# Side work queued by products, and three of four sums of weight quarters made by adding transfers, in a three-layer fp32 block kernel

## The reference

```python
h = rms_norm(x, pre_norm[layer])
c_b, c_c, c_x, c_z, r_q, r_k, r_v, r_z = split(h @ w_in[layer])      # 8 x 1024 columns
y_conv = c_b * causal_depthwise_conv(c_c * c_x, conv_w[layer]) * silu(c_z)
q, k = apply_rotary(r_q), apply_rotary(r_k)                          # 8 heads of 128
ret = retention_chunkwise(q, k, r_v, log_gamma)                      # chunks of 128 tokens
y_ret = ret * rsqrt(mean(ret * ret) + eps) * silu(r_z)
x = x + rms_norm(concat(y_conv, y_ret) @ w_out[layer], post_norm[layer])
```

## Time and profile before

| | us |
|---|---|
| median of 3 runs | 1948.93 |
| lowest, highest | 1947.12, 1953.82 |
| profiled execution, its own time | 1956.33 |
| its span | 1954.2 |

### The profile page before, as it was taken

How to read it: one execution, slowest core, us unless ns; L and a number is a source line. 1 busy time by engine, 2 the same in 40 slices (tenths; PEclk the granted TensorE clock), 3 DMA queues, 4 the chain that set the end, 5 groups by cost and what they waited for, 6 DMA issues and landing times.

```text
span 1954.2 us, 32772 instructions
## 1 busy us (share of the span) xinstructions
PE 1861.4 (95%) x13846; PEld 1760.0 (90%) x13846; DVE 1385.4 (71%) x2461; ACT 903.4 (46%) x1731; POOL 1.2 (0%) x9
## 2 busy tenths in 40 slices
PE   8999999999999999998999999998998898989898
PEld 7999999777999989996889999997898898989887
DVE  5888896577666744666787878876378868786854
ACT  5223333677544422434355555555356455545442
POOL 0000000000000000000000000000000000000000
PEclk9999999999999999999999999998999899999999
DMA  5222222110222232322222222222222222222231
GB/s 183 87 87 87 87 88 86 44 44 22 87 93 87 71 121 90 100 70 83 74 74 78 87 87 87 87 87 87 87 87 66 65 87 80 94 66 87 87 117 67
DMA packets 151856, 163.91 MB, mean 84 GB/s; under 512 B 3494, under 2 KB 148191, under 8 KB 151710
## 3 DMA queue, kind: packets, MB, share of 16 engines
q1 hardware_dynamic: 151694, 161.82, 25.8%
q10 hardware_dynamic: 16, 0.00, 0.0%
HBM read 159.71 MB, written 2.10 MB: 83 GB/s over the span
## 4 chain that ended last, share of the span: by engine, by line
PE 77%; DVE 15%; ACT 5%; issue 2%; DMA 0%; DVEq 0%; SPq 0%; ACTq 0%
PE ps L195 63%; PE ps L199 12%; DVE wlo L210 4%; PE ps L204 2%; ACT ones_d L207 2%; ACT whi L207 1%; DVE raw L210 1%; DVE pa L210 1%; DVE xa L218 1%; DVE sz L218 1%; DVE xa L210 1%; DVE na L210 1%; DVE na L218 1%; DVE rcol L218 1%; DVE s1t L210 1%
## 5 line engine op out<-in xcount | busy, mean ns | idle before, releaser
L210 DVE TENSOR_TENSOR wlo<-raw,whi 128x1024 fp32r<-128x1024 f32 (+1 forms) x352 | 417.1, 1192 | 335.8 <-ACT whi L207 334.8
L207 ACT ACTIVATE whi<-raw 128x1024 fp32r<-128x1024 f32 (+1 forms) x352 | 359.7, 1032 | 227.8 <-PE ps L195 205.4
L195 PE MATMUL ps<-nhi,whi 128*128 128x256 f32 (+3 forms) x1824 | 401.0, 288 | 11.1 <-DVE wlo L210 7.7
L195 PE MATMUL ps<-nhi,wlo 128*128 128x256 f32 (+3 forms) x1824 | 397.4, 286 | 0.0
L195 PE MATMUL ps<-nlo,whi 128*128 128x256 f32 (+3 forms) x1696 | 360.1, 286 | 0.0
L195 PEld LDWEIGHTS ps<-nhi,whi 128*128 128x128 f32 x1824 | 294.4, 190 | 15.1 <-DVE wlo L210 8.3
L195 PEld LDWEIGHTS ps<-nhi,wlo 128*128 128x128 f32 x1824 | 293.4, 190 | 1.6
L195 PEld LDWEIGHTS ps<-nlo,whi 128*128 128x128 f32 x1696 | 268.9, 190 | 1.5
L199 PE MATMUL ps<-thi,whi 128*128 128x256 f32 x704 | 209.4, 298 | 9.4 <-DVE wlo L210 4.4
L199 PE MATMUL ps<-tlo,whi 128*128 128x256 f32 x704 | 203.6, 289 | 0.0
L199 PE MATMUL ps<-thi,wlo 128*128 128x256 f32 x704 | 203.5, 289 | 0.0
(11 more groups left out here) (310 smaller groups left out, 3305.6 us busy)
## 6 DMA issues: line engine op xcount, KB each, us to landing
raw<-in_w_in_dram SPq DMA_DIRECT2D x90, 1024.0 KB, 5.3
raw<-in_w_up_dram SPq DMA_DIRECT2D x22, 1024.0 KB, 5.1
raw<-in_w_out_dram SPq DMA_DIRECT2D x20, 1024.0 KB, 5.0
raw<-in_w_down_dram SPq DMA_DIRECT2D x8, 768.0 KB, 4.3
raw<-in_w_down_dram SPq DMA_DIRECT2D x8, 640.0 KB, 4.0
raw<-in_w_conv_out_dram SPq DMA_DIRECT2D x4, 1024.0 KB, 5.0
xt<-in_x_dram SPq DMA_DIRECT2D x4, 512.0 KB, 5.5
raw<-in_w_in_dram SPq DMA_DIRECT2D x4, 512.0 KB, 8.2
```

Source lines behind the costliest of these rows:

```text
L195: return pe.put(after, lambda e: e.matmul(o, w, m, start=start, stop=stop_), mark)
L207: return ac.put(after, lambda e: e.activation(o, i, func, **kw))
L210: return dv.put(after, lambda e: e.tensor_tensor(o, a, b, op))
```

## The change

Two things are done, both in the retention layers.

**Sums.** `S1T` becomes two buffers. `quarter_sums(u, t)` is now called by `load`, right behind the load of the unit: SP loads w21 again from DRAM into `S1T[i]`; a POOL transfer with `accum_op=add` adds w22 from DRAM to it (t1); a second adds w11 from DRAM to w21 in the unit's buffer (t3). `second_sum` is called at the low split of slot a: a third adding transfer adds `S1T[i]` to w11, inside SBUF (t2). `fourth_sum`, on DVE as before, is called at the low split of slot b. Who waits for whom is as before.

**Queueing.** `prep` makes at most one low and one high split a call. `tick(n)`, called once per product of `seven`, once per k-tile of v and z, and once per k-tile of `mix_out`'s first pair, runs what `after_beats` has set for this beat, then `prep`, then `n` loose entries; the four `fill(s0 + 8)` are gone, and `slot(i)` fills only if a slot isn't ready. `scores`, `states`, `mix_values`, `turn_back`, `turn_residual`, `leave_v` and `leave_z` issue their PE part at once and their ACT and DVE parts one to four beats later; five pieces stand one to four hooks elsewhere (8 to 7, 15 to 16, 18 to 14, 20 to 19, and the residual's 22, 24 to 20, 22). The loose entries of the two halves of a unit are interleaved. `mix_split` is parted into `mix_high` and `mix_low`.

```diff
-    def dma(self, after, dst, src, count):
+    def dma(self, after, dst, src, count, **kw):
         token = count.up(16)
-        self.ops.append((list(flat(after)), lambda e: e.dma_start(dst, src), count.sem, 16))
+        self.ops.append((list(flat(after)), lambda e: e.dma_start(dst, src, **kw), count.sem, 16))
...
-        S1T = at("s1t", [128, 4, 128], F, o_raw + 2 * 8192)
-        WHI.append(at("whi4", [128, 512], R, o_raw + 2 * 8192 + 2048))
-        WLO.append(at("wlo4", [128, 512], R, o_raw + 2 * 8192 + 4096))
+        S1T = [at(f"s1t{i}", [128, 4, 128], F, o_raw + 2 * 8192 + 2048 * i) for i in range(2)]
+        WHI.append(at("whi4", [128, 512], R, o_raw + 2 * 8192 + 4096))
+        WLO.append(at("wlo4", [128, 512], R, o_raw + 2 * 8192 + 6144))
...
             loaded[u] = {k: t for k in range(src.shape[1])}
+            if plan[u][1] is SEVEN:
+                quarter_sums(u, t)
...
-        def quarter_sums(u):
-
-
+        s1_of, s1_used = {}, [[], []]
+        c_s0, c_s1, c_s2, c_s3 = [[Count(sem(f"{n}{i}")) for i in range(2)] for n in ("q", "qa", "qb", "qc")]
+
+        def quarters_of(u):
             raw = RAW[rawbuf[u]].rearrange("p (k c) -> p k c", k=KT)
-            w11, w21, w12, w22 = raw[:, 0:4, 0:128], raw[:, 0:4, 128:256], raw[:, 4:8, 0:128], raw[:, 4:8, 128:256]
-            t1 = tt([loaded[u][0], summed.get("split"), ready[-1][2]], S1T, w21, w22, ALU.add)
-            t3 = tt([t1], w21, w11, w21, ALU.add)
-            t2 = tt([t1, t3], w11, w11, S1T, ALU.add)
-            t4 = tt([t2], w12, w12, w11, ALU.add)
-            summed[u] = {1: t1, 2: [t2, t3], 3: t4}
+            return raw[:, 0:4, 0:128], raw[:, 0:4, 128:256], raw[:, 4:8, 0:128]
+
+        def quarter_sums(u, t_raw):
+
+
+            assert first_layer + 4 <= u
+            i = s1_of[u] = len(s1_of) % 2
+            src = plan[u][0]
+            t = sp.dma([s1_used[i], summed["split"]], S1T[i], src[:, 0:4, 128:256], c_s0[i])
+            t1 = po.dma([t], S1T[i], src[:, 4:8, 128:256], c_s1[i], accum_op=ALU.add)
+            t3 = po.dma([t_raw], quarters_of(u)[1], src[:, 0:4, 0:128], c_s3[i], accum_op=ALU.add)
+            summed[u] = {1: t1, 2: [t3]}
+
+        def second_sum(u, after):
+
+            i = s1_of[u]
+            t2 = po.dma([after, summed[u][1]], quarters_of(u)[0], S1T[i], c_s2[i], accum_op=ALU.add)
+            summed[u][2].append(t2)
+            s1_used[i] = [t2]
+
+        def fourth_sum(u):
+
+            w11, _, w12 = quarters_of(u)
+            summed[u][3] = tt([summed[u][2]], w12, w12, w11, ALU.add)
...
-                assert len(ready) == s
-                quarter_sums(u)
-                raw = S1T
+                raw = S1T[s1_of[u]]
...
-            if len(box) > 4 and box[4] == 1 or rawbuf[u] == 2:
+            if rawbuf[u] == 2:
                 summed["split"] = t_lo
+            if len(box) > 4:
+                if box[4] == 0:
+                    second_sum(u, t_lo)
+                elif box[4] == 1:
+                    s1_used[s1_of[u]].append(t_lo)
+                elif box[4] == 2:
+                    fourth_sum(u)
             if last and follows[u]:
                 load(follows[u], [t_lo])
...
+        def prep():
+
+            if len(ready) < len(halves):
+                split_lo(len(ready))
+            s = len(halves)
+            if s < len(slots) and slots[s][0] in loaded and (before[s] is None or before[s] in gone):
+                split_hi(s)
+
+        posts, beat = {}, [0]
+
+        def after_beats(n, f):
+            posts.setdefault(beat[0] + n, []).append(f)
+
+        def tick(n):
+
+            beat[0] += 1
+            for f in posts.pop(beat[0], []):
+                f()
+            prep()
+            loose_run(n)
...
-                    fill(s0 + 4)
-                    (ah, al, ta), (ch, cl, tc), (bh, bl, tb), (dh, dl, td) = ready[s0:s0 + 4]
+
+                    def slot(i):
+                        fill(s0 + i + 1)
+                        return ready[s0 + i]
+
+                    ah, al, ta = slot(0)
...
-                    fill(s0 + 8)
                     hook(1)
+                    bh, bl, tb = slot(2)
                     t = t_used[0] = product(A, bh[:, :, left], bl[:, :, left], tb, summed_(0), False, True, s1)
                     u2 = act([t], d12, A, ACT.Copy)
                     hook(2)
+                    ch, cl, tc = slot(1)
                     t = t_used[1] = product(C, ch, cl, tc, summed_(1), True, True, claim(banks[2]))
                     done(t, s0 + 1)
                     k5 = act([t, after[1]], d22, C, ACT.Copy)
-                    fill(s0 + 8)
                     hook(3)
                     t = t_used[2] = product(A, bh[:, :, right], bl[:, :, right], tb, summed_(2), False, True, u2)
                     done(t, s0 + 2)
                     u3 = act([t], d21, A, ACT.Copy)
                     c22 = stt([k5, u3], d22, d22, -1.0, d21, ALU.mult, ALU.subtract)
-                    fill(s0 + 8)
                     hook(4)
+                    dh, dl, td = slot(3)
...
-                def mix_split(*ks):
+                def mix_high(*ks):
                     for k in ks:
-                        a = act([t_mx[k], t_used[k // 4]], MXH[:, k, :], MXF[:, k, :], ACT.Copy)
-                        mtok[k] = [a, tt([a], MXL[:, k, :], MXF[:, k, :], MXH[:, k, :].bitcast(F), ALU.subtract)]
+                        mtok[k] = [act([t_mx[k], t_used[k // 4]], MXH[:, k, :], MXF[:, k, :], ACT.Copy)]
+
+                def mix_low(*ks):
+                    for k in ks:
+                        mtok[k].append(tt(mtok[k], MXL[:, k, :], MXF[:, k, :], MXH[:, k, :].bitcast(F), ALU.subtract))
...
+                                if k == half[-1]:
+                                    done(tk)
+                                tick(3)
...
-                    pieces = {1: lambda: scores(0), 4: lambda: states(0), 8: lambda: mix_values(0), 12: lambda: scores(1),
-                              15: lambda: states(1), 18: lambda: turn_back(0), 20: lambda: mix_values(1), 26: lambda: turn_back(1)}
+                        def leave():
+                            t_mx[k] = act([tk, t_t], MXF[:, k, :], P[:, z:z + 512], ACT.Copy)
+                            release(t_mx[k], r1)
+
+                        after_beats(1, leave)
+
+                    pieces = {1: lambda: scores(0), 4: lambda: states(0), 7: lambda: mix_values(0), 12: lambda: scores(1), 14: lambda: turn_back(0),
+                              16: lambda: states(1), 19: lambda: mix_values(1), 26: lambda: turn_back(1)}
                     if l:
-                        pieces[22] = lambda: turn_residual(p, 0, r1, t_t)
-                        pieces[24] = lambda: turn_residual(p, 1, r1, t_t)
-                    def x_out(c, t):
-                        t_xa[c] = tt([t, st["r2"]], XA[c], XA[c], R2, ALU.mult)
+                        pieces[20] = lambda: after_beats(1, turn_residual(p, 0, r1, t_t))
+                        pieces[22] = lambda: after_beats(1, turn_residual(p, 1, r1, t_t))
...
                         def hook(m, n=n):
+                            tick(2)
                             if 7 * n + m in pieces:
                                 pieces[7 * n + m]()
-                            loose_run(2)
                             if p == 3 and n == 3 and m >= 3:
-                                mix_split(*[None, None, None, (0, 1), (2, 3), (8, 9), (10, 11)][m])
+                                if m > 3:
+                                    mix_low(*early[m - 4])
+                                mix_high(*early[m - 3])
...
-                        loose_run(len(loose))
                         zs = [bank_dst(b) for b in banks]
+                        for n, ks in enumerate(((4, 5), (12, 13), (6, 7), (14, 15))):
+                            after_beats(2 * n + 1, lambda ks=ks: mix_high(*ks))
+                            after_beats(2 * n + 2, lambda ks=ks: mix_low(*ks))
                         for i, n in enumerate((0, 2, 1, 3)):
-                            slot = take()
-                            if n in (1, 3):
-                                mix_split(*range(4 * n, 4 * n + 4))
-                            t = list(products(slot, range(4 * n, 4 * n + 4), MXH, MXL, mtok, [d for _, d, _ in zs],
-                                              [claim(b) for b in banks], i == 0, i == 3))
-                            done(t[1])
+                            fill(taken[0] + 1)
+                            slot = ready[taken[0]]
+                            taken[0] += 1
+                            for k in range(4 * n, 4 * n + 4):
+                                t = list(products(slot, [k], MXH, MXL, mtok, [d for _, d, _ in zs], [claim(b) for b in banks],
+                                                  i == 0 and k == 0, k == 15, base=k % 4))
+                                if k % 4 == 3:
+                                    done(t[1])
+                                tick(2)
```

(85 more changed lines are left out.)

41 lines of the change are left out of this document (20 added, 21 removed).

## The result

| | us |
|---|---|
| kernel after, median of 4 runs | 2186.57 (2181.65 to 2187.62) |
| kernel before beside it | 1948.99 |
| ratio | 1.121, interval 1.1183 to 1.1236 |
| span of the profiled execution | 2184.8 (before 1954.2) |

The account below looks back on a forecast made before the run. No single resource bounds it; DVE, through ACT, holds back PE in the seven-product stretch. Loop +137, remainders -32 and mix -6 make +99 us: 2055 us profiled, 2048 at the median, range 1930 to 2150.

Parts of the forecast that it names:

- the loop: Successive seven-product units: t2 waits on POOL behind the next unit's loads, delaying the splits that issue the following raw load; +137 us.
- Rival 1: POOL and its transfers are cheap, a turn takes 14.1 to 14.5 us; 1940 us at the median; chance 0.12.
- Rival 2: The loop does not bind in the seven-product units and DVE's relief comes through; about 1903 us; chance 0.12.
- rival 4: ACT and DVE find old work in a worse order, PE waits for PSUM copies; +62 us, 2011 us; chance 0.07.
- T: Length of one turn of the loop, raw load to raw load in seven-product units: 17.3 us, 36 times.
- raw issue until S1T's first sum is issued: Start of the turn: raw load lands after 5.3 us, S1T's load behind it 0.9 us later, together 6.2 us.
- two issues on POOL: In the turn, t1 and t3 of the next unit hold POOL ahead of t2 for 1.0 us each.
- t2, issue to landing: In the turn, the second sum's adding transfer: 3.0 us as a 256 KB load plus one more pass of 0.9, 3.9 us.
- splits and fourth sum, with handovers: End of the turn: b's high and low splits, the fourth sum, d's high and low splits, 5.25 us.
- Rival 3: The forecast's mechanism with slow POOL, T of 20.5 us or more; +214 us, 2163 us; chance 0.09.
- the sum of the 36: Present total of the 36 raw-load intervals that the loop would hold, in both retention layers: 486 us before the change.
- the remainders of the six chains of five: The k, v, z rest after five looped raw loads: 34.6 us falls by 4; over all eight chains -32 us.

Follow-up runs that it names:

- run 1: Changed kernel with t1 and t3 of the next unit put on POOL behind t2 of the present unit, same transfers; 1959.62 us, 1.0019 of the kernel before.
- run 3: Kernel before, with its old queueing, given the changed kernel's three adding transfers in place of three sums on DVE; 2198.41 us, 1.1235 of the kernel before.
- run 5: Changed kernel with only t3 of the next unit put behind t2 on POOL, t1 and its wait staying ahead; 2132.05 us, 1.0905 of the kernel before.
- run 6: Changed kernel with the second sum made by DVE at slot a's low split, t1 and t3 still adding transfers; 1897.08 us, 0.9703 of the kernel before.
- run 2: Changed kernel with all four sums on DVE again, the new queueing by products kept; 1945.82 us, 0.9952 of the kernel before.
- run 7: Run 2's kernel with the second head's scores, states and mix_values, plus turn_back(0) and the residual, one or two hooks later; 1907.90 us, 0.9761 of the kernel before.
- run 4: Changed kernel with the three adding transfers made plain copies of the same bytes, weight sums not made; 2078.55 us, 1.0623 of the kernel before.

## Why the prediction was wrong

**The direction and the mechanism held.** t2 stands behind two waits on POOL, the loop closes, and it has the members named: the chain of the changed kernel lists them one by one, and runs 1, 3, 5 and 6 open, keep or shorten it as it says. Rivals 1 and 2 (cheap POOL, no loop) fell, as did rival 4: run 2 is under the kernel before, though run 2 against 7 shows its kind of mishap, 38 us of it, in the side work. PE's slower clock was rightly priced at nothing: its 58 us more of busy time lie inside the longer turns.

**The step that failed is the length of the turn, T.** Term by term, prediction against the kernel after (one turn of its chain, 1131.58 to 1151.36, 19.8 us):

| term | predicted | measured |
|---|---|---|
| raw issue until S1T's first sum is issued | 6.2 | 6.7 |
| two issues on POOL | 2.0 | 1.5 |
| t2, issue to landing | 3.9 | 6.3 |
| splits and fourth sum, with handovers | 5.25 | 5.4 |
| turn | 17.3 | 19.8 here, 20.3 in the mean of 36 |

The term that was mis-sized is t2's landing, 3.9 us in the sum and 6.4 in the median. It was priced as if it were alone on the rings (the core's 16 DMA engines) with one pass more. Instead it queues behind two adding transfers issued 0.75 and 1.5 us before it. With none ahead it lands after 4.7 us (run 1), behind one after 5.8 (run 5), behind two after 6.4; as the last of three copies after 3.7 (run 4). So some 0.8 us of the error is the adding transfer by itself and 1.7 the two ahead of it. Slices of the turn have the rate, the raw load in the first, the adding transfers in the others:

```profile
1135.00:1136.00 1.00, 1.00 (x7) 1.00 (x6) 0.00 (x0) 0.14 (x1) 0.00 (x0) 0.50 1.07 376
...
1141.00:1142.00 1.00, 1.00 (x11) 1.00 (x10) 0.00 (x0) 0.00 (x0) 1.00 (x1) 1.00 1.41 172
1142.00:1143.00 1.00, 1.00 (x11) 1.00 (x10) 0.00 (x0) 0.00 (x0) 0.14 (x1) 1.00 1.13 128
1143.00:1144.00 1.00, 0.59 (x6) 0.40 (x4) 0.00 (x0) 0.00 (x0) 0.00 (x0) 1.00 1.43 179
```

The share of the rings is above 1 (it adds up packet times, which overlap) at 128 to 179 GB/s, where the raw load of the same turn moved 376. Rival 3, given 0.09, had the length, T = 20.5, but by luck: it put 3.0 us on each issue, which took 0.75, and 3.0 on t2's landing, which took over twice that. The bounds were laid on the issue and on a landing without others, not on what is ahead on the rings. The 3.0 us that T was short are 36 x 3.0 = 108 of the 139 us that the forecast missed.

**Two smaller errors.** I read the phase of the raw loads two issues late. The changed kernel marks it (its S1T loads tell the units apart): a chain begins with the load for c, and before the change the chain of this group runs from 1073.91 to 1137.69, 63.8 us, not 65.6; the sum of the 36 is 479, not 486. So the intervals grew by 732 - 479 = 253 us, and all the rest gave back 23 (the span grew by 230.6), not 38: the remainders of the six chains of five took 34.2 us in the mean against 35.9, 1.7 less and not 4. The error of 139 us is then accounted for within 2: 108 for T, 7 for the sum of the 36, 15 for what was not given back, and 7 because the profiled execution before was that much above its median and the one after was not.

**What would have shown it.** The prediction named ACT's wait of several microseconds a unit (8), PE under 38 of 50 us (37.86, 32.02), DVE under 35 (19.20, 23.77) and a clock under 0.95 (0.83, 0.87), and all came. Its spacing of 15 to 19.5 us did not (19.7 to 20.5 in this group, up to 22.0 in others), nor did the 31 us for the loads of the remainder (33.7 to 36.2).

**The page's fit.** The fit of the Trainium skill, "DMA: Bandwidth & Descriptors", section "Anatomy of one DMA", of 2.0 us plus bytes over 436 GB/s, gives an estimate of 2.6 us for a POOL transfer of 256 KB. The measurements decide against it here: copies by POOL took 3.4 to 3.7 with others beside them (run 4), adding ones 4.6 and more in the median.

## What to carry to other kernels

Before work is moved to a queue that runs in order, write that queue down over two iterations: a ready operation behind a wait for a fresh load puts the load's whole latency into every iteration, and here the order alone was worth 227 us (run 1). Give transfers the results with an iteration of slack, keep on the engine the one that is wanted soon, and price each transfer by what is ahead of it on the rings. When a producer is delayed by beats, move the reader of its bank by as many.

## What the runs showed of the hardware

- An adding transfer of 256 KB in 512-byte rows landed 4.7 us after its issue with no other adding one ahead (run 1, median), a copy by POOL 3.7 as the last of three (run 4). The page's packet counts of POOL's queue differ too, for the same 34.61 MB: 69696 packets adding (13.1% of the engines' span), 10560 copying (5.8%).
- POOL issued three transfers 0.75 us apart. The records of adding ones last 1.28, 1.84 and 2.40 us and overlap; those of copies last 0.75.
- They did not slow DVE's low splits of 1024 columns in run 6, where 36 of 201 of them overlap a record of POOL: their mean is 1219 ns, that of the others 1222. In the kernel after only three overlap, so that its mean (1193 ns in all forms, 1192 before) says nothing of this.
